# Far-block masks moved ahead of the rope products of the next queries on VectorE

## The reference, cut to what matters

```
xa, ga, q, k, v, gb, gm = split_columns(h @ w_in)
y_a = pool_mixer(xa, ...) * silu(ga)             # branch A: windowed means
q, k = apply_axial_rope(q), apply_axial_rope(k)  # products with cos and sin
p = softmax([scores over own/neighbour keys, masked to +-128, context keys, sink])
y_b = (p @ v) * silu(gb)                         # branch B, 16 heads, 4 key heads
merged = sigmoid(gm_a) * (y_a @ w_a) + sigmoid(gm_b) * (y_b @ w_b)
out = x + gate * rms_norm(merged @ w_out)
```

## Time and profile before

| | |
|---|---|
| median of three runs | 2377.49 us |
| the profiled execution's own time | 2375.37 us |
| its span (first to last instruction, slowest core, core 5) | 2373.8 us |
| spans of the eight cores | 2366.8 to 2373.8 us |
| busy: PE / DVE / ACT / POOL | 2257.8 / 1595.3 / 1150.0 / 773.6 us |
| mean granted TensorE clock of the cores | 0.988 to 0.992 |

### The profile page before, as it was taken

The page is one execution under the profiler, slowest core; times in us unless marked ns, Lnnn a source line. Parts: engine busy times, 40 slices in busy tenths (PEclk is TensorE's granted clock), DMA queues, the critical chain, the costliest instruction groups (busy, mean ns, idle before and its releaser), DMA issues.

```text
span 2373.8 us, 67010 instructions; the slowest of 8 cores (2366.8 to 2373.8 us)
## 1 busy us (share of the span) xinstructions
PE 2257.8 (95%) x23952; PEld 1336.5 (56%) x23952; DVE 1595.3 (67%) x4226; ACT 1150.0 (48%) x2341; POOL 773.6 (33%) x982
## 2 busy tenths in 40 slices
PE   6789999999999999999999999999999999999998
PEld 1466555555555556556556555555555655655554
DVE  0466776676676676676677667677667667766765
ACT  1255445545545544544544544544554454454453
POOL 0233333233233233233233333333323333333332
PEclk9899999999999999999999999999999999999999
DMA  9981332233232233232234233224223223322212
GB/s 245 222 158 52 69 86 68 68 79 68 70 77 68 70 77 68 70 77 68 70 77 81 69 74 81 70 65 86 68 71 77 68 70 77 73 69 74 72 49 63
DMA packets 234314, 193.77 MB, mean 82 GB/s; under 512 B 197492, under 2 KB 205812, under 8 KB 231432
## 3 DMA queue, kind: packets, MB, share of 16 engines
q1 hardware_dynamic: 231544, 168.45, 29.3%
q0 software_dynamic: 2448, 21.04, 4.8%
HBM read 125.02 MB, written 33.56 MB: 67 GB/s over the span
## 4 chain that ended last, share of the span: by engine, by line
PE 83%; DVE 9%; issue 3%; ACT 2%; DMA 2%; POOL 1%; DVEq 0%; another core or an unknown queue 0%; SPq 0%; ACTq 0%; POOLq 0%
PE pb L581 27%; PE pb L588 22%; PE pb L934 9%; PE pb L876 8%; PE pb L830 5%; PE pb L773 5%; PE pb L868 5%; DMA s_PT<-x 2%; DVE s_hT L540 2%; DVE s_Gb L712 2%; DVE s_yb L839 2%; ACT s_ttmp L711 2%; DVE s_PT L812 1%; PE pb L359 1%; POOL s_mg L880 1%
## 5 line engine op out<-in xcount | busy, mean ns | idle before, releaser
L581 PE MATMUL pb<-s_W,s_hT 128*128 128x512 bf16 (+1 forms) x3584 | 776.4, 366 | 0.0
L588 PE MATMUL pb<-s_hT,s_W 128*128 128x128 bf16 x9216 | 600.3, 220 | 64.0 <-DVE s_hT L540 62.4
L588 PEld LDWEIGHTS pb<-s_hT,s_W 128*128 128x128 bf16 x9216 | 531.3, 98 | 175.7 <-issue 137.9
L802 ACT ACTIVATE s_PT<-pb 128x512 bf16<-128x512 f32 x1024 | 529.0, 608 | 117.5 <-PE pb L773 116.9
L581 PEld LDWEIGHTS pb<-s_W,s_hT 128*128 128x128 bf16 x3584 | 340.0, 98 | 312.6 <-issue 5.3
L857 ACT ACTIVATE s_Tm<-pb 128x512 bf16<-128x512 f32 x256 | 153.2, 599 | 389.3 <-PE pb L581 195.0
L812 DVE TENSOR_TENSOR s_PT<-s_PT,s_maskb 128x512 bf16<-128x512 bf16 (+1 forms) x384 | 296.7, 786 | 45.2 <-ACT s_PT L802 22.8
L880 POOL TENSOR_TENSOR s_mg<-s_ub,s_scr 128x512 bf16<-128x512 f32 x128 | 162.1, 1266 | 341.0 <-DVE s_scr L861 337.4
L690 DVE TENSOR_TENSOR s_scr<-pb,s_ropet 128x512 f32<-128x512 f32 x256 | 165.0, 686 | 133.6 <-PE pb L588 133.6
L876 PE MATMUL pb<-s_wmf,s_ybT 128*128 128x512 bf16 x1024 | 242.6, 380 | 0.0
L839 DVE SCALAR_TENSOR_TENSOR s_yb<-pb,s_small,s_Gb 128x64 bf16<-128x64 f32 x1024 | 220.3, 277 | 29.2 <-DVE s_small L836 2.2
(11 more groups left out here) (125 smaller groups left out, 2461.9 us busy)
## 6 DMA issues: line engine op xcount, KB each, us to landing
s_xr<-x SPq DMA_DIRECT2D x63, 512.0 KB, 4.1
y<-s_xr SPq DMA_DIRECT2D x63, 512.0 KB, 2.8
s_xt<-x SPq DMA_DIRECT2D x62, 512.0 KB, 4.1
s_W<-w_in POOLq DMA_DIRECT2D x10, 1024.0 KB, 31.6
s_ropet<-rope SPq DMA_DIRECT2D x64, 128.0 KB, 2.5
s_wmf<-w_mod SPq DMA_DIRECT2D x2, 2048.0 KB, 13.2
s_W<-w_mod SPq DMA_DIRECT2D x2, 2048.0 KB, 28.1
s_wmf<-w_mod POOLq DMA_DIRECT2D x2, 2048.0 KB, 18.4
```

Source lines behind the costliest of these rows:

```text
L581: E("pe", lambda e, k=k: e.matmul(out=pb[:, c0:c0 + n], lhsT=h[:, k, :], rhs=W[:, wblk, k, c0:c0 + n], start=(k == 0), stop=(k == 7)), rea ...
L588: E("pe", lambda e, c=c, k=k: e.matmul(out=pb[:, c * 128:(c + 1) * 128], lhsT=W[:, wblk, k, c * 128:(c + 1) * 128], rhs=h[:, k, :], start= ...
L802: E("act", lambda e, g=g: e.activation(out=PT[:, jb, g, :], in_=banks[g][0][:, :], func=AF.Exp, scale=0.125), reads=[banks[g][1]], writes= ...
```

## The change

The loop over `pend` moves out of `vis()` into a function `masks()`, which `vis()` calls, and `masks()` is called once more, between `out_evac` and `norm_sq`. At that point `pend` holds the far visit. So the four far masks are emitted before `norm_sq` and `P_q` instead of behind them. The next `vis()` finds `pend` empty.

```
-            def vis():
+            def masks():
                 for m in pend:
                     mask(p, m)
                 pend.clear()
+
+            def vis():
+                masks()
                 jb = next(visits, None)
...
             if hasO:
                 out_evac(p - 2, so)
+            masks()
             if nxt:
                 norm_sq()
             q = P_q(p + 1) if hasP else iter(())
```

## The result

| | before | changed |
|---|---|---|
| median of the runs | 2377.88 us (6 runs) | 2277.39 us (2277.01 to 2277.80, 6 runs) |
| span of the profiled execution | 2373.8 us | 2275.8 us (core 4) |
| periods 4 to 62, mean | 35.18 us | 33.56 us |
| busy DVE | 1595.3 us | 1494.4 us |

The ratio of the runs is 0.9579, with a 95% interval of 0.9566 to 0.9592: 4.2% faster, 2277 us against 2280 forecast.

A forecast was written before the change was run, and what follows sets the result against it. PE bounds, waiting each period for DVE's L540, delayed through the far masks. Gains of 88.5, 4.7 and 5.0 us make 98; 2375.4 - 98 = 2277.4, and the median 2.1 above: about 2280 us, range 2268 to 2318.

The forecast's parts named there:

- The mechanism: Far masks beside L695 delay L861, L880, the `pv` evacuations, L719, L711, L712 and L540, for which PE waits.
- main term: PE's loss at the start of a period falls by 1.50 us, in 59 periods 88.5 us.
- left of PE's loss a period: At L588, chunk 7 ready at 1271.96 against 1271.82 wanted, so 0.13 us still lost.
- The cost of the masks: Four far masks on DVE take 1.73 us in the new place, with 3.38 as the other bound.
- The place of the wait: L711 on ACT starts 0.14 us after DVE's L719 ends, both tanh sharing `s_ttmp`; PE's L581 does not release it.
- the 1.63 us: PE's loss at a period's start: L588 to L581 takes 2.54 us in a steady period against 0.91 with chunks in time.
- The total of 98 us: Expected gain: 88.5 us from the periods, 4.7 from the mean wait's excess, 5.0 from the clock.
- The excess of the mean wait: PE's mean idle is 1.06 us and not 0.98; 0.08 x 59 = 4.7 us goes too.
- The lower end of the range, 2268: The forecast's own lower end: all of 1.67 + 0.13 us regained, and the clock.
- the 1.67 us: Expected shortening of PE's whole period, from 35.18 us to 33.5.
- The clock's 5 us: Behind three of the longest waits TensorE's clock was low for some 8 us; 1.7 us each, 5.0 in all, goes.
- The slower rival: Masks keep 3.38 us in the new place, all behind is 0.16 late: 9.4 us slower, 2387 us; chance 7%.

The follow-up runs named there:

- experiment 1: Changed kernel plus three POOL additions of 420 elements, which read SBUF, beside the far masks in each steady period: 2388.1 us, 1.0036 of before.
- experiment 2: Changed kernel plus five POOL memsets of 420 elements, which read nothing, beside the far masks: 2278.84 us, 0.9579 of before.
- Experiment 6: Kernel before, with the tanh of `ga` in a free `s_Tm` buffer instead of `s_ttmp`, so L711 need not wait for L719: 2312.94 us, 0.9726 of before.
- experiment 4: Kernel before, with POOL's two L695 emitted behind the far masks and made to wait for them: 2457.71 us, 1.0329 of before.
- experiment 5: Kernel before plus one DVE memset of 480 elements between L712 and the second four L540, in 62 periods: 2422.33 and 2423.15 us, 1.0190 of before.

## Why the prediction was right

The mechanism was right, link by link, and the size came out by its main term. Point by point, in the period shown above, measured times taken back by 14.22 us to the clock of the earlier trace rows:

| step | forecast | measured |
|---|---|---|
| far masks start | 1252.2 | 1252.19 |
| masks, start to next start | 1.73 us | 1.73 us |
| second L690 pair | 1255.30 | 1255.18 |
| L695, both | 1256.13 to 1258.82 | 1256.01 to 1258.51 |
| L861 into `s_scr` | 1257.6 | 1257.43 |
| L880 | 1258.85 | 1258.46 |
| L861 into `s_ub` | 1260.23 | 1260.02 |
| L861 into `s_scr`, second | 1266.1 | 1266.12 |
| L719 | 1268.6 | 1268.72 |
| L711 | 1269.46 | 1269.56 |
| second four L540 | 1270.84 | 1270.93 |
| left of PE's loss a period | 0.13 us | 0.10 to 0.24, in 8 of 58 periods 0.38 to 0.48 |

- *The cost of the masks* was read from the last period, where POOL is idle, and held. Experiments 1 and 2 show why. The 0.87 us that the prediction calls the cost of a mask in a steady period is a mean of two masks of some 1.25 us beside L695 and two of 0.42.
- *The place of the wait.* That L719 and not L581 held L711 was an argument from the earlier trace rows and from when the matmuls were done. Experiment 6 shows it.
- *The loss is larger than the idle time.* 62.4 us stood in the waits; the 59 periods became 95.4 us shorter, of which some 90 are the usual period, 35.02 to 33.50. Counting from start to start gave the 1.63 us; by the idle time alone the forecast would have been 2315.
- *The total of 98 us came in part by luck.* The span is 98.0 us shorter, as summed, but two terms were off. The excess of the mean wait, put at 4.7 us, did not go: the mean of the periods without a fall of the clock lay 0.06 us above the usual one before and lies 0.06 above it now, because in 18 of 58 periods PE still loses 0.15 to 0.48 us. In its place 2.6 us were won outside the 59 periods, which the sum put at nothing. The lower end of the range, 2268, counts the clock twice, since the 1.67 us already hold it.
- *Two sizes on the path were off and cancelled.* L695 takes 2.50 us and not the 2.69 that I kept from the earlier trace rows: the masks had slowed POOL too. So L880 ended early, and L861 into `s_ub` waited for PE's L868. Behind it the `pv` train took 6.10 us and not 5.87, waiting for matmuls.
- *The clock's 5 us.* No period of the changed kernel is over 33.9 us on any core, so the three slow stretches went. The 8 us of the earlier trace rows hold the wait itself; by the periods' lengths each fall cost 1.7 us beyond its longer wait. Experiments 4 and 5 show that they come with these waits more and more often as the waits grow; that a wait causes a fall is shown by them, what decides in a single period is not.
- *The slower rival was mis-sized in kind.* Its 9 us were met by experiment 1, but from other parts, as said there. A longer wait costs more than its length: with L880 0.39 us late, experiment 4 is 80 us slower, where the rival's way of counting gives 23.

## What to carry to other kernels

Look for two engines that take turns without a semaphore between them: the same instruction with a duration of 0.42 us at one place and 1.3 at another (L812 beside an idle POOL and beside L695) is such a place, and so is L540 with 0.31 and 1.32 (beside L880). Look at single durations, not at a mean over the line. Moving such an instruction by a few places can be free time, as it was for the masks; for L540 it was not tried. Follow a wait of the bounding engine back through buffers that are shared (`s_ttmp`, `s_scr`, `s_ub`) by the ends of what was read and written, not by the releaser's name alone, and price it from start to start. A move pays only while the whole path behind it has room: the same edit of L540 brought PE to its floor where `ya` had room, and ran into a new wait that cost 0.8 us a period where it had not.

## What the runs showed of the hardware

- A DVE minimum with both inputs in SBUF is held by a POOL instruction that reads SBUF, and holds it in turn: 1.82 us for four alone, 3.82 beside three POOL additions, which take 3.52 instead of 2.7. POOL memsets beside it change nothing (1.82).
- A DVE multiply-add with one tensor input in SBUF and two scalars a partition (L540) took 1.32 us beside POOL's L880 and 0.31 otherwise, in 58 periods of each of the two kernels. That L880 is the cause rests on where the long one stands and ends; no run removed L880.
- TensorE's granted clock was 0.77 to 0.79 on average over stretches of 7.3 to 8 us that hold a wait of 1.3 to 1.6 us (1.00 in a window in the middle of a period), and each fall cost some 1.7 us of work. On the longest core it fell in 3, 8, 22 and 42 of 59 periods with mean waits of 1.06, 1.15, 1.36 and 1.45 us, and in none of the changed kernel. In this kernel, a wait of 1 us in every period was near the point from which more waiting is paid twice.
